# Splits ahead of the norms, squares in summed buffers, and the last recurrent block's first half ahead of its second

## The reference

```python
def rmsnorm(x, g):
    return x * rsqrt(mean(x * x, axis=-1) + EPS) * g

# layer 0, the recurrent mixer, in 4 blocks of 256 features
proj = rmsnorm(h) @ w_in;  gate_branch, rec = proj[..., :1024], proj[..., 1024:]
rec = causal_depthwise_conv(rec, conv_w, conv_b)          # 4 taps
gate_i, gate_r = sigmoid(rec_block @ w_gates + b_gates)   # per block
log_a = -8 * gate_r * softplus(-lru_param)
a = exp(log_a);  u = rec * gate_i * sqrt(1 - a * a)
h_t = a_t * h_(t-1) + u_t                                 # a scan over the tokens
h = h + (gelu(gate_branch) * h_scan) @ w_out
# after each mixer
h = h + (silu(xn @ w_gate) * (xn @ w_up)) @ w_ffn_out
```

## Time and profile before

| | |
|---|---|
| median of 3 runs | 2488.86 us |
| the profiled execution, its own time | 2491.47 us |
| its span in the trace | 2489.7 us |
| mean granted TensorE clock | 0.991 of full |
| PE busy | 2419.5 us, 97% |
| DVE busy | 1276.4 us, 51% |
| ACT busy | 789.3 us, 32% |
| POOL busy | 117.4 us, 5% |
| a 512 KB weight load, median from issue to landing | 3.3 to 5.2 us |

### The profile page before, as it was taken

How to read it: one execution, slowest core, us unless ns; L and a number is a source line. 1 busy time by engine, 2 the same in 40 slices (tenths; PEclk the granted TensorE clock), 3 DMA queues, 4 the chain that set the end, 5 groups by cost and what they waited for, 6 DMA issues and landing times.

```text
span 2489.7 us, 28279 instructions
## 1 busy us (share of the span) xinstructions
PE 2419.5 (97%) x11273; PEld 1985.9 (80%) x11273; DVE 1276.4 (51%) x1256; ACT 789.3 (32%) x1062; POOL 117.4 (5%) x77
## 2 busy tenths in 40 slices
PE   7899989999999999998999999989999999999998
PEld 5688867888888888877888888877788888888887
DVE  4767764334444433457666666653433444443345
ACT  3443562111111111144666666643211111111113
POOL 1000000000000000021111111101000000000000
PEclk9999999999999999999999999999999999999999
DMA  4110111111111111120111111021211111111111
GB/s 119 60 51 25 51 34 43 51 51 46 46 51 48 45 51 51 52 93 18 35 35 34 34 34 34 26 93 51 68 51 51 51 42 51 51 42 51 51 43 68
DMA packets 167289, 123.13 MB, mean 49 GB/s; under 512 B 5080, under 2 KB 148672, under 8 KB 167232
## 3 DMA queue, kind: packets, MB, share of 16 engines
q1 hardware_dynamic: 165504, 118.04, 15.6%
q10 hardware_dynamic: 1728, 4.31, 0.7%
HBM read 113.89 MB, written 8.45 MB: 49 GB/s over the span
## 4 chain that ended last, share of the span: by engine, by line
PE 89%; DVE 6%; ACT 3%; issue 2%; POOL 0%; DMA 0%; ACTq 0%; DVEq 0%
PE ps L694 65%; PE ps L970 9%; PE ps L1017 3%; PE ps L1100 3%; PE ps L1004 3%; PE ps L736 1%; PE ps L985 1%; PE ps L982 1%; DVE rstd L1544 1%; PE ps L1079 1%; PE ps L943 1%; DVE wl L1512 1%; DVE tmp L1592 0%; PE ps L1048 0%; PE ps L984 0%
## 5 line engine op out<-in xcount | busy, mean ns | idle before, releaser
L1551 DVE TENSOR_TENSOR tmp<-ps,rstd 128x1024 f32<-128x1024 f32 x96 | 117.2, 1224 | 509.0 <-PE ps L694 508.9
L1557 DVE TENSOR_TENSOR resid<-ps,resid 128x1024 f32<-128x1024 f32 x204 | 247.2, 1222 | 165.8 <-PE ps L694 165.7
L694 PE MATMUL ps<-xh,wh 128*128 128x512 f32 x976 | 307.9, 397 | 17.8 <-DVE wl L1512 12.7
L1148 ACT ACTIVATE wh<-raw 128x1024 fp32r<-128x1024 f32 x192 | 200.8, 1050 | 389.0 <-PE ps L694 354.9
L1512 DVE TENSOR_TENSOR wl<-raw,wh 128x1024 fp32r<-128x1024 f32 x192 | 242.8, 1267 | 150.4 <-ACT wh L1148 150.3
L694 PE MATMUL ps<-xl,wh 128*128 128x512 f32 x976 | 303.7, 393 | 0.0
L694 PE MATMUL ps<-xh,wl 128*128 128x512 f32 x976 | 303.0, 392 | 0.0
L694 PEld LDWEIGHTS ps<-xh,wh 128*128 128x128 f32 x976 | 184.1, 190 | 61.9 <-issue 18.4
L694 PE MATMUL ps<-x1h,wh 128*128 128x512 f32 x704 | 218.3, 391 | 3.3 <-DVE wl L1512 2.1
L694 PE MATMUL ps<-x1l,wh 128*128 128x512 f32 x704 | 216.8, 389 | 0.0
L694 PE MATMUL ps<-x1h,wl 128*128 128x512 f32 x704 | 216.7, 389 | 0.0
(11 more groups left out here) (226 smaller groups left out, 3491.2 us busy)
## 6 DMA issues: line engine op xcount, KB each, us to landing
raw<-in_w_ffn_in SPq DMA_DIRECT2D x88, 512.0 KB, 3.8
raw<-in_w_ffn_out SPq DMA_DIRECT2D x44, 512.0 KB, 3.3
raw<-in_w_rec_in SPq DMA_DIRECT2D x16, 512.0 KB, 5.2
raw<-in_w_kvf SPq DMA_DIRECT2D x16, 512.0 KB, 3.9
xin<-in_x SPq DMA_DIRECT2D x4, 1024.0 KB, 9.8
raw<-in_w_rec_out SPq DMA_DIRECT2D x8, 512.0 KB, 4.2
raw<-in_w_q SPq DMA_DIRECT2D x8, 512.0 KB, 3.9
spill<-resid SPq DMA_DIRECT2D x8, 512.0 KB, 2.6
```

Source lines behind the costliest of these rows:

```text
L694: last = pe.matmul(acc[:, h], w, v[:, h], start=(first and p == 0), stop=(final and p == 2))
L1148: act.activation(wh[slot][:, :], raw[slot][:, :], ACT.Copy).then_inc(hi_ready[slot], 1)
L1551: dve.tensor_tensor(dst, ps[slot][:, :], rstd[:, :], ALU.mult).then_inc(drained[slot], 1)
L1557: dve.tensor_tensor(resid[:, m, :], ps[slot][:, :], resid[:, m, :], ALU.add).then_inc(drained[slot], 1)
```

## The change

It has four parts.

1. `SQ_BUF` gives the squares of tiles 0 to 7 the buffers 0, 1, 2, 3, 1, 3, 3, 0. Squares 4 to 6 wait for the pair sums on POOL (`sq_summed`), square 7 waits for the first `stat` on PE. This holds for all four norms.
2. In `start`, the split of pieces `recA` 2 and 3 and the LRU constants stand ahead of mean, root and reciprocal.
3. In `recE` and `attE`, the split of piece 2 of the next stage stands ahead of mean, root and reciprocal.
4. In the last recurrent block DVE's order is changed: a gate tile is scaled ahead of a weight split in two places, the first half's `lru_output` stands ahead of the second half's multiplication, and the low part of y's first half (`last_y_low(0)`) ahead of the second half's `lru_output`. ACT makes the high part of y's first half between exp and square root of the second half.

```diff
+    SQ_BUF = [0, 1, 2, 3, 1, 3, 3, 0]
-            return (sq_att if seg == "attE" else ffn_tmp[seg == "ffn1E"])[k % 4][:, :]
+            return (sq_att if seg == "attE" else ffn_tmp[seg == "ffn1E"])[SQ_BUF[k]][:, :]
...
-                if k >= 4:
-                    act.wait_ge(sq_used, STAT[seg] * (SUMS - 1) + k // 2 - 1)
+                if 4 <= k < 7:
+                    act.wait_ge(sq_summed, STAT[seg] * PAIR_SUMS + k - 3)
+                elif k == 7:
+                    act.wait_ge(sq_used, STAT[seg] * (SUMS - 1) + 1)
...
+            split_hi(pieces.use("recA", 2), None)
+            act.wait_ge(lru_step, 1)
+            act.activation(lru[:, 1, :], lru[:, 0, :], ACT.Exp).then_inc(lru_step, 1)
+            act.wait_ge(lru_step, 3)
+            act.activation(lru[:, 3, :], lru[:, 2, :], ACT.Ln).then_inc(lru_step, 1)
+            split_hi(pieces.use("recA", 3), (in_filled, 1))
             root("start")
...
+                if between is not None:
+                    between()
                 act.activation(at[1][:, :], at[1][:, :], ACT.Sqrt, bias=TINY).then_inc(lru_act, 1)
...
+            def last_y_high(t):
+                act.wait_ge(y_ready, (BLOCKS - 1) * 2 + (t + 1))
+                act.activation(ch[:, t, :], gelu[:, t, :], ACT.Copy).then_inc(yh_ready, 1)
+
             lru_gates("recZ", 7, b, 0, LRU_LAST[0])
-            lru_gates("recZ", 7, b, 1, LRU_LAST[1])
+            act.wait_ge(lru_dve, b * 10 + 3)
+            lru_gates("recZ", 7, b, 1, LRU_LAST[1], lambda: last_y_high(0))
             split_hi(pieces.use("recE", 0), REC_END[0])
-            act.wait_ge(lru_dve, b * 10 + 4)
-            for t in range(2):
-                act.wait_ge(y_ready, b * 2 + (t + 1))
-                act.activation(ch[:, t, :], gelu[:, t, :], ACT.Copy).then_inc(yh_ready, 1)
+            last_y_high(1)
...
             epilogue("recE", [lambda: split_hi(pieces.use("ffn0A", 0), FFN_START[0][0]),
-                              lambda: split_hi(pieces.use("ffn0A", 1), FFN_START[0][1])])
+                              lambda: split_hi(pieces.use("ffn0A", 1), FFN_START[0][1])],
+                     lambda: split_hi(pieces.use("ffn0A", 2), FFN_START[0][2]))
...
+            split_hi(pieces.use("ffn1A", 2), FFN_START[1][2])
             root("attE")
...
             conv("recZ", b, 0)
+            gate_scaled("recZ", b, 0)
             split_lo(pieces.use("recZ", 4, b))
-            split_lo(pieces.use("gates", 0, b))
             conv_low(b, 0)
-            gate_scaled("recZ", b, 0)
             last_add(0)
             conv("recZ", b, 1)
+            split_lo(pieces.use("gates", 0, b))
...
+            lru_sum(0, LRU_LAST[0])
+            lru_input("recZ", 7, b, 0, LRU_LAST[0], b * 10 + 1)
+            lru_sum(1, LRU_LAST[1])
+            lru_output(b, 0, LRU_LAST[0], b * 10 + 3)
             last_add(3)
+            lru_input("recZ", 7, b, 1, LRU_LAST[1], b * 10 + 3)
+            last_y_low(0)
             lru_output(b, 1, LRU_LAST[1], b * 10 + 7)
             split_lo(pieces.use("recE", 0))
+            last_y_low(1)
```

82 lines of the change are left out of this document (37 added, 45 removed).

## The result

The changed kernel takes 2465.7 us (median of 4 runs, 2465.1 to 2467.0) against 2487.8 us (2486.4 to 2491.4) for the kernel before in the same set of runs: a ratio of 0.991, 95% interval 0.9893 to 0.9927. It is faster by 22 us. The prediction was 2465.

What follows compares the result with a forecast made beforehand. PE, busy 97% of the span, bounds the kernel, so only its waits and slow stretches can be won. 11.9 + 5.7 + 3.8 + 2.1 = 23.5 us off 2491.5 gives 2468.0, carried to the median 2465; range 2459.5 to 2471.5, 8 in 10.

Steps and rivals of the forecast that it cites:

- squares: In start, new square buffers let PE end the last stat at 54.5 instead of 61.05: 6.6 us.
- order, with the split between the convolutions: In start, splits and constants ahead of the mean give 5.6 us, one split less between the convolutions 2.1.
- clock behind the new wait: Slow PE restart behind a 6.1 us wait ahead of block 0's gates: 2.4 us lost, bounds 0 and 2.5.
- start in all: All gains up to the gates of block 0, 14.3 us, less 2.4 for the clock: 11.9 us.
- last block: Last recurrent block: PE restarts for recE 0 at 342.1 instead of 347.77, 5.7 us won.
- clock behind the last block's wait: Slow restart stands behind the last block's wait before and after, so it cancels (bounds -1 and +1).
- norm behind the mixer: At recE the 2.14 us wait and the 1.7 us slow restart go: 3.8 us.
- norm behind attention: At attE the 2.14 us wait goes, with no slow restart behind it: 2.1 us.
- Rival (a): In start, POOL's third sum and DVE hold each other, squares come late, 6.6 us lost: 2472; 5%.
- Rival (b): Inside the blocks, a piece of block 1 comes late and start's 11.9 us are lost: 2477; 4%.
- Rival (c): Last block's first half is enough for PE, which goes on at 336.4, 5.7 us more: 2460; 3%.
- Rival (e): PE stays at 1.2 GHz long after the gates' or last block's wait; 60 us would give 2495; 2%.

Runs made afterwards that it cites:

- e2: Kernel before with only the splits of recA 2 and 3 and the LRU constants moved ahead of the first mean: 2481.7 us, ratio 0.9967.
- e10: Kernel before with only the last recurrent block's gate tiles scaled ahead of the weight splits: 2484.4 us, ratio 0.9988.
- e3: Kernel before with only piece 2 split ahead of the mean at the norms behind mixer and attention: 2483.1 us, ratio 0.9968.
- e4: Kernel before with only the new order of the last recurrent block: 2481.5 us, ratio 0.9967.
- e9: Changed kernel with the first half's y split late again, behind recE 0: 2466.4 us, ratio 0.9910 to before.
- e5: Changed kernel with the low part of recE 0 made behind the first product of the second output: 2461.1 us, ratio 0.9881 to before.
- e1: Kernel before with only the new square buffers: 2485.2 us, ratio 0.9981.
- e7: Changed kernel with 24 unused matmuls in PE's wait ahead of block 0's gates: 2463.9 us, ratio 0.9888 to before.
- e8: Changed kernel with recE 0 split earlier, first gates piece ahead of the mean, its tile in PSUM buffer 1, and 16 fill matmuls: 2455.8 us, ratio 0.9860 to before.
- e12: The kernel of e8 timed again, no edit, in another set of runs: 2455.8 us, ratio 0.9869 to before.

## Why the prediction was right, step by step

The sum was 23.5 us on the profiled execution, and 24.4 were measured. Its terms against the landmarks (the start's own, up to PE's tile in the last block, is 301.01 to 289.20, where 301.01 is the 302.51 of the earlier trace rows less its 1.50 us wait):

| step | predicted | measured | from |
|---|---|---|---|
| squares | 6.6 | 6.8 | 61.08 to 54.24 |
| order, with the split between the convolutions | 7.7 | 7.65 | mean to gates 35.68 to 28.03 |
| clock behind the new wait | -2.4 | -2.7 to -3.0 | 14.49 less 11.81; 0.51 over 6.2 us |
| start in all | 11.9 | 11.8 | 301.01 to 289.20 |
| last block | 5.7 | 5.6 | 17.41 less 11.81 |
| clock behind the last block's wait | 0 | 0.6 | 18.03 less 17.41 |
| norm behind the mixer | 3.8 | 4.0 | 22.05 less 18.03 |
| norm behind attention | 2.1 | 2.4 | 24.5 less 22.05 |

**The squares.** The rows foretold are all there. The timeline of ACT in `start` of the kernel after:

```profile
26.02 1.04 ACT L1173 ACTIVATE tmp<-resid 128x1024 f32<-128x1024 f32 x1
...
30.14 1.04 ACT L1173 ACTIVATE tmp<-resid 128x1024 f32<-128x1024 f32 x1
...
33.70 1.06 ACT L1173 ACTIVATE tmp<-resid 128x1024 f32<-128x1024 f32 x1 [0.32 <-POOL tmp L655]
```

The square of tile 4 ends at 27.1 (foretold 27.4), where the earlier trace rows had 12.93 us of wait, and that of tile 5 at 31.2 (31.4). The meeting of POOL's third sum and DVE came, once, as priced. First the sum, then DVE's low halves around it, and the mean:

```profile
31.26 2.41 POOL L655 TENSOR_TENSOR tmp<-tmp 128x1024 f32<-128x1024 f32 x1 [4.43 <-ACT tmp L1173]
```

```profile
28.97 1.27 DVE L1535 SCALAR_TENSOR_TENSOR xl<-resid,vec,xh 128x1024 fp32r<-128x1024 f32 x1
...
32.11 2.64 DVE L1535 SCALAR_TENSOR_TENSOR xl<-resid,vec,xh 128x1024 fp32r<-128x1024 f32 x1
...
54.24 1.23 DVE L1546 TENSOR_SCALAR rstd<-ps 128x1024 f32<-128x1024 f32 x1 [2.37 <-PE ps L737]
```

The low half of tile 5 took 2.64 us beside the sum and 1.27 without it, and was through at 34.75, ahead of the 35.7 allowed; the mean starts at 54.24, for 54.5. Rival (a) needed a second meeting, which did not come. The Trainium skill ("SBUF — State Buffer", the glossary of terms) has the loser blocked for the whole instruction: the half would then run from 33.67, the sum's end, to 34.9, and the trace agrees within 0.2 us.

What the step did not say is what the 6.6 us are made of. The list of PE's waits of before has a line that went with the old buffers, the wait for tile 5, and behind it stands a slow stretch:

```profile
PE ps L694 <- DVE xl L1529: 3.5, 1, 3.5
```

```profile
42.70:48.90 6.20, 6.13 (x13) 4.46 (x14) 3.33 (x3) 0.68 (x1) 2.24 (x1) 0.50 0.00 0
```

The step counted PE's work behind the first `stat` at full clock, and so took in both: 3.5 us of wait and 3.1 of clock. The second is not there in every execution. From the start of the first `stat` to the mean it is 23.70 us in before, 23.64 and 23.71 in e2 and e10, but 22.37 and 22.41 in e3 and e4, which lost 1.7 us behind the same wait; with the new buffers it is 17.09 or 17.10 in all nine. So the squares are worth 6.6 us or 5.3.

**The order.** 5.6 and 2.1 us were foretold, and 7.65 came in the change and 7.66 in e2. That the long wait does not vanish but leaves some 6.1 us ahead of the gates (6.29 measured) was read from PE's own work behind the last `stat`. The splits lie ahead of the mean, and DVE waits there:

```profile
50.65 1.23 DVE L1518 TENSOR_TENSOR wl<-raw,wh 128x1024 fp32r<-128x1024 f32 x1 [4.01 <-ACT wh L1149]
```

It waits for PE by way of ACT, whose high part needs the slot (foretold to be free at 49.7):

```profile
49.49 1.06 ACT L1149 ACTIVATE wh<-raw 128x1024 fp32r<-128x1024 f32 x1 [5.32 <-PE ps L695]
```

The low part ends at 51.9 (foretold 52), and the 2.37 us wait of the mean above is its slack.

**Rival (b), given back inside the blocks.** The chain of the kernel after has one piece from the gates to the last block (start, us, what), where the earlier trace rows had 152.59 us:

```profile
56.59 6.57 DVE rstd L1550
...
82.27 223.43 PE ps L695 x972
...
378.48 682.78 PE ps L695 x3012
```

Gates to PE's tile in the last block is 206.93 us after and 204.25 before; the 2.7 more are the slow clock at its start. Nothing else was given back.

**The last block.** ACT takes the two halves as foretold. The timeline of ACT and that of DVE, after:

```profile
305.72 1.12 ACT L1224 ACTIVATE tmp<-ps,vec 128x1024 f32<-128x1024 f32 x1 [0.69 <-PE ps L695]
...
319.56 1.04 ACT L1286 ACTIVATE ch<-gelu 128x1024 fp32r<-128x1024 f32 x1
...
321.91 1.06 ACT L1235 ACTIVATE lru_alt<-lru_alt 128x1024 f32<-128x1024 f32 x1
```

```profile
323.01 1.23 DVE L1650 SCALAR_TENSOR_TENSOR lru_alt<-lru_alt 128x1024 f32<-128x1024 f32 x1 [0.78 <-ACT lru_alt L1235]
...
329.00 1.22 DVE L1518 TENSOR_TENSOR wl<-raw,wh 128x1024 fp32r<-128x1024 f32 x1
```

Sigmoid i waits 0.69 us for PE (0.8 foretold). The second root ends at 322.97; foretold was 334.8 less the start's gain of 11.8, 323.0. From there to the end of the split is 7.25 us (5.98 + 1.2 foretold). The wait of 5.64 us was put at some 5.7. Rival (c), that the first half would be enough for PE, was out by the order, and e9 and e5 show that the piece was what held it: y alone early gives nothing (2466.4 to 2466.2), y and piece early give 4.6 to 5.1 of the 5.7 us that (c) named. One claim of the step was idle: the early y, told as a part of the gain, was not needed for it. The 5.6 us are 3.3 of scaling (e10) and the rest of halves in the other order.

**The norms.** The waits of 2.14 us went at both. At `recE` the clock came back as foretold (1.00 in the third stretch row above; e3's 4.1 us). At `attE` the profile of before had no slow stretch behind its 2.14 us, in e1 the same wait had one (0.72 over 6.0 us, 1.7 lost); so the term is 2.1 in one execution and 3.8 in another.

**The clock.** The term of 2.4 for the new wait was of the right sign and near in size: 3.0 in the profile shown, 2.84 in e7's difference, 1.7 in e5's profile. The 3.0 is beyond the bound of 2.5 that was set. The bound came from four restarts; one more in the trace of before, at 42.77, lost 3.1 us over 6.1 (the row above) and would have given a wider one. Rival (e), a clock that stays low, did not come. In the last block the same allowance, taken to cancel, gave 0.6.

Nor are short waits free of it. e8 and e12 are one and the same kernel in two executions. At one place in attention, behind a wait of 1.22 us in both and in code that the change does not touch, first e8, then e12:

```profile
1601.10:1607.10 6.00, 5.87 (x35) 4.80 (x36) 4.63 (x9) 3.33 (x8) 0.00 (x0) 1.00 0.77 285
```

```profile
1599.40:1605.40 6.00, 5.96 (x27) 5.06 (x28) 4.26 (x7) 2.81 (x7) 0.00 (x0) 0.72 0.80 282
```

One lost nothing, the other 1.7 us. At the same place before lost 1.7 us (0.72 over 6.0) and e4 nothing (1.00). The profile of before fell near the upper end of its runs, which is why the gain of the profiles (24.4) is larger than that of the medians (22.1). The range of 2459.5 to 2471.5 allowed for it by its four restarts. That the forecast came within 1 us of the median is in part luck: the mechanisms and the waits were right to some 0.4 us, but four of the terms have clock time in them that comes and goes by 1 to 3 us each.

## What to carry to other kernels

Ask of every wait what the engine has queued behind the step before it: the same weight split, late by the same order, cost 10.3 us where nothing was left for PE and 2.1 where three terms were; moving it gave the whole 2.1, but only 7.7 of the 10.3, since the next supplier was late behind it. A wait costs twice where the TensorE clock falls behind it, so a wait that can't be removed can still be made cheaper by harmless matmuls in it (e7: 2.8 us on the path, 2.0 on the median), and cutting one to about a microsecond kept the clock in e5, if not everywhere. Moving one of two things that PE needs is worth nothing while the other stays late (e9, and e5 for both). And a kernel with one part changed can seem to gain what the clock gave it: e2 and e4 came out 3 us better than the places that they edit, so the gain of a part is read at its place.
